# Sample attention: scores for four pages at once as rows instead of page by page as columns, key norms turned instead of scores, sequences written out on every engine

## The reference, cut to what matters

```python
k_nope = jnp.einsum('blc,chn->blhn', c, w_uk)
k = rms_norm(jnp.concatenate([k_nope, k_pe], axis=-1), g)
s = jnp.einsum('bqhd,blhd->bhql', q, k) * SM_SCALE
p = jax.nn.softmax(jnp.where(mask, s, -jnp.inf), axis=-1)
o_lat = jnp.einsum('bhql,blc->bqhc', p, c_all)
```

## Time and profile before

| | us |
|---|---|
| median of 3 runs | 3951.54 (3949.32 to 3975.61) |
| the profiled execution | 3975.4 |
| its span, first to last instruction | 3973.6 |
| PE busy, share of the span | 3224.3 (81%) |
| DVE busy | 2961.7 (75%) |
| ACT busy | 1041.3 (26%) |
| POOL busy | 1579.9 (40%) |
| mean granted PE clock, 1.0 is full speed | 0.872 |

### The profile page before, as it was taken

The page is one execution under the profiler, slowest core; times in us unless marked ns, Lnnn a source line. Parts: engine busy times, 40 slices in busy tenths (PEclk is TensorE's granted clock), DMA queues, the critical chain, the costliest instruction groups (busy, mean ns, idle before and its releaser), DMA issues. The chain is left out here.

```text
span 3973.6 us, 57296 instructions
## 1 busy us (share of the span) xinstructions
PE 3224.3 (81%) x19892; PEld 2722.2 (69%) x19892; DVE 2961.7 (75%) x5977; ACT 1041.3 (26%) x1915; POOL 1579.9 (40%) x1320
## 2 busy tenths in 40 slices
PE   6653787886999996665663768999999999999997
PEld 3443444654555554335662658999999999999997
DVE  3247686586665663775998996888888888888887
ACT  2221122222222221111212553222222222223221
POOL 0035354365333331663656772333333333333332
PEclk9577897576988997777886898999999999999998
DMA  2221775477876765882000338888888888888886
GB/s 105 102 92 39 273 266 198 136 256 247 262 248 219 230 197 172 306 321 81 27 17 23 158 152 296 307 300 300 294 297 296 296 291 294 304 300 293 292 301 237
DMA packets 303823, 876.76 MB, mean 221 GB/s; under 512 B 34009, under 2 KB 125450, under 8 KB 292554
## 3 DMA queue, kind: packets, MB, share of 16 engines
q0 software_dynamic: 147456, 536.94, 39.5%
q1 hardware_dynamic: 154170, 334.15, 23.4%
q10 hardware_dynamic: 2016, 3.67, 0.3%
HBM read 819.17 MB, written 55.74 MB: 220 GB/s over the span
## 5 line engine op out<-in xcount | busy, mean ns | idle before, releaser
L110 POOL DMA_INDIRECT x_got<-v,x_expert x512 | 548.9, 1072 | 969.1 <-DVE x_y L131 868.9
L110 POOL DMA_INDIRECT x_got<-u_rows,x_expert x512 | 566.6, 1107 | 854.6 <-DVE x_got L124 734.2
L131 DVE SCALAR_TENSOR_TENSOR x_y<-x_got,x_hidden,x_y 128x1024 f32<-128x1024 f32 x512 | 666.4, 1302 | 39.8 <-DMA x_got<-v,x_expert 29.9
L124 DVE SCALAR_TENSOR_TENSOR x_got<-x_got,x_y 128x1024 f32<-128x1024 f32 x512 | 621.1, 1226 | 37.8 <-DMA x_got<-u_rows,x_expert 36.1
L1682 PE MATMUL e_a<-h2h,e_uh 128*128 128x272 f32 x2048 | 591.0, 289 | 21.4 <-DVE e_ul L1760 20.8
L1684 PE MATMUL e_a<-h2h,e_ul 128*128 128x272 f32 x2048 | 594.3, 290 | 0.0
L1699 PE MATMUL e_y<-e_wh,e_vh 128*128 128x272 f32 x2048 | 588.3, 287 | 3.6 <-DVE e_wl L1783 3.6
L1683 PE MATMUL e_a<-h2l,e_uh 128*128 128x272 f32 x2048 | 589.6, 288 | 0.0
L1700 PE MATMUL e_y<-e_wl,e_vh 128*128 128x272 f32 x2048 | 588.2, 287 | 0.0
L1701 PE MATMUL e_y<-e_wh,e_vl 128*128 128x272 f32 x2048 | 587.3, 287 | 0.0
L1682 PEld LDWEIGHTS e_a<-h2h,e_uh 128*128 128x128 f32 x2048 | 386.6, 189 | 22.2 <-issue 21.1
(11 more groups left out here) (382 smaller groups left out, 5693.3 us busy)
## 6 DMA issues: line engine op xcount, KB each, us to landing
e_u<-uT SPq DMA_DIRECT2D x128, 512.0 KB
e_v<-v SPq DMA_DIRECT2D x64, 1024.0 KB
gates_d<-g_stage SPq DMA_DIRECT2D x8, 4352.0 KB
e_gate<-gates_d SPq DMA_DIRECT2D x32, 1088.0 KB
d_page<-page SPq DMA_DIRECT2D x128, 144.0 KB
d_latent<-page_rows SPq DMA_DIRECT2D x128, 128.0 KB
t0r_w<-w_pq SPq DMA_DIRECT2D x16, 512.0 KB
x_got<-u_rows,x_expert POOLq DMA_INDIRECT x512
```

What stands on the lines that cost most here:

```text
L110: pool.indirect_dma_start(out=self.got[n % RING_G][:], out_offset=None, in_=self.tables[phase], in_offset=bass.IndirectOffsetOnAxis(ap=sel ...
L124: dve.scalar_tensor_tensor(out=row[:], in0=row[:], scalar=1.0, in1=self.y[g][:], op0=ALU.mult, op1=ALU.mult, accum_out=self.hidden[:, g, k ...
L131: dve.scalar_tensor_tensor(out=self.y[g][:], in0=row[:], scalar=self.hidden[:, g, k:k + 1], in1=self.y[g][:], op0=ALU.mult, op1=ALU.add).t ...
```

## The change

- **Scores by rows.** After each fourth page PE makes the scores of four pages at once (`group`): the queries are the weights (128 by 32, and 32 by 32 for the rotary part), and four pages of keys are 512 columns. The result is 32 rows by 512 in one of two banks `sc`, which ACT copies to the score row (`raw`). The per-page matmuls into `st` and DVE's copies of them are gone.
- **Norms turned.** The reciprocal norms are spread to 32 columns for each page (`kinv`), and PE turns these instead of the scores, by matmuls with the identity. DVE multiplies the score row by them, bank by bank (`scaled`), before pages 2 and 3 of the next sequence.
- **New keys.** They are read in place; `k_new` and its copy are gone. The score row exists twice.
- **Loops.** All engines have the 8 sequences written out, with constant addresses.
- **Loads.** SP loads the next keys after the rotary squares and the fourth `raw` copy.

```diff
-        qr = sb("d_qr", [ROPE, H, NS])
-        qa = sb("d_qa", [P, CT, H, NS])
+        qr = sb("d_qr", [ROPE, DEC_B * SQ])
+        qa = sb("d_qa", [P, CT, DEC_B * SQ])
...
-        s_all2 = [sb(f"d_s{e}", [P, PAGES + 1, SQ]) for e in range(2)]
-        rows = sb("d_rows", [P, PAST + DEC_S])
-        s_row = rows[0:SQ, :]
+        kinv = sb("d_kinv", [P, PAGES, SQ])
+        s_new = [sb(f"d_snew{e}", [DEC_S, SQ]) for e in range(2)]
+        rows = [sb(f"d_rows{e}", [P, PAST + DEC_S]) for e in range(2)]
+        s_row = [r[0:SQ, :] for r in rows]
...
-        st = [bank("d_st0"), bank("d_st1")]
+        sc = [bank("d_sc0"), bank("d_sc1")]
...
+        def sequences(pages, tail):
+
+
+
+            before = {}
+            for b in range(DEC_B):
+                pages(b, b % 2, b // 2 + 1, before)
+                before = tail(b, b % 2, b // 2 + 1)
+            for step in before.values():
                 step()
...
-            with sp.Fori(0, DEC_B // 2 - 1) as m:
-                for e in range(2):
-                    n = 2 * m + e + 1
-                    sp.wait_ge(s["d_s1"], n)
-                    load_keys(n + 1, e)
-                    sp.wait_ge(s["d_lat"], n)
-                    load_latents(n + 1, e)
+            for n in range(1, DEC_B - 1):
+                e = (n - 1) % 2
+                sp.wait_ge(s["d_krsq"], n)
+                sp.wait_ge(s["d_raw"], GROUPS * n)
+                load_keys(n + 1, e)
+                sp.wait_ge(s["d_lat"], n)
+                load_latents(n + 1, e)
...
+                def group(c):
+
+                    after(pe, s["d_raw"], GROUPS * b + c - 1)
+                    o = sc[c % 2][0:SQ, :].rearrange("q (p l) -> q p l", l=P)
+                    four = slice(4 * c, 4 * c + 4)
+                    for k in range(CT):
+                        pe.matmul(o, qa[:, k, some], page[e][:, four, k * P:(k + 1) * P], start=k == 0, stop=False)
+                    pe.matmul(o, qr[:, some], krT[e][:, four, :], start=False, stop=True).then_inc(s["d_sc"], 1)
...
-                    after(pe, s["d_sev"], b * PAGES + p - 1)
                     for k in range(CT):
-                        pe.matmul(kn[p % 2][:, :], page[e][:, p, k * P:(k + 1) * P], w_uk[:, k, :],
-                                  start=k == 0, stop=k == CT - 1)
-                    for k in range(CT):
-                        pe.matmul(st[p % 2][:, 0:SQ].rearrange("p (h t) -> p h t", t=DEC_S),
-                                  page[e][:, p, k * P:(k + 1) * P], qa[:, k, :, cols], start=k == 0, stop=False)
-                    mm = pe.matmul(st[p % 2][:, 0:SQ].rearrange("p (h t) -> p h t", t=DEC_S),
-                                   krT[e][:, p, :], qr[:, :, cols], start=False, stop=True)
+                        mm = pe.matmul(kn[p % 2][:, :], page[e][:, p, k * P:(k + 1) * P], w_uk[:, k, :],
+                                       start=k == 0, stop=k == CT - 1)
                     mm.then_inc(s["d_mm"], 1)
+                    if p % 4 == 3:
+                        group(p // 4)
...
-                        pe.wait_ge(s["d_knew"], b + 1)
                         after(pe, s["d_smask"], b)
                         for h in range(H):
-                            mm = pe.matmul(new[0:DEC_S, h * DEC_S:(h + 1) * DEC_S], k_new[:, h, :],
-                                           qk_s[0:HD, h, bass.ds(b * DEC_S, DEC_S)], start=True, stop=True)
+                            mm = pe.matmul(new[0:DEC_S, h * DEC_S:(h + 1) * DEC_S], qk_s[0:HD, H + h, cols],
+                                           qk_s[0:HD, h, cols], start=True, stop=True)
...
-                def turn_first():
-
-                    pe.wait_ge(s["d_s1"], t + 1)
+                def norms_first():
+
+                    pe.wait_ge(s["d_kinv"], t + 1)
+                    after(pe, s["d_olT"], t)
+                    after(pe, s["d_pt"], 2 * t)
+                    norms(0)
+                    norms(1)
+
+                def norms(c):
+                    for p in range(4 * c, 4 * c + 4):
+                        mm = pe.matmul(misc[c % 2][0:SQ, (p % 4) * P:(p % 4 + 1) * P], kinv[:, p, :], ident[:],
+                                       start=True, stop=True)
+                    mm.then_inc(s["d_tr"], 1)
+
+                def norms_rest():
+                    for c in (2, 3):
+                        pe.wait_ge(s["d_nb"], GROUPS * t + c - 1)
+                        norms(c)
                     pe.wait_ge(s["d_smask"], t + 1)
-                    pe.wait_ge(s["d_olT"], t)
-                    pe.wait_ge(s["d_pt"], 2 * t)
-                    turn(0)
...
-                        mm = pe.transpose(misc[c % 2][0:SQ, (p % 4) * P:(p % 4 + 1) * P], s_all[:, p, :], ident[:])
-                    mm.then_inc(s["d_tr"], 1)
-
-                def turn_rest():
-                    for c in (2, 3):
-                        pe.wait_ge(s["d_row"], 5 * t + c - 1)
-                        turn(c)
-                    pe.transpose(new[0:SQ, 2 * SQ:2 * SQ + DEC_S], s_all[0:DEC_S, PAGES, :],
-                                 ident[0:DEC_S, 0:DEC_S]).then_inc(s["d_tr"], 1)
+                    pe.transpose(new[0:SQ, 2 * SQ:2 * SQ + DEC_S], s_new[e][:],
+                                 ident[0:DEC_S, 0:DEC_S]).then_inc(s["d_ntr"], 1)
...
-                return {1: turn_first, 2: turn_rest, 6: probs, 7: latent, 9: latent_turn}
-            sequences(pe, lambda b: None, pages, tail)
...
+                    if p % 4 == 3:
+                        c = p // 4
+                        act.wait_ge(s["d_sc"], GROUPS * b + c + 1)
+                        after(act, s["d_ptr"], 2 * (b - 1))
+                        act.activation(s_row[e][:, 512 * c:512 * c + 512], sc[c % 2][0:SQ, :],
+                                       ACT.Copy).then_inc(s["d_raw"], 1)
...
-                    act.activation(s_row[:, 512 * c:512 * c + w],
-                                   misc[c % 2][0:SQ, 0:w] if c < 4 else new[0:SQ, 2 * SQ:2 * SQ + w],
-                                   ACT.Copy).then_inc(s["d_row"], 1)
...
+                def row_new():
+                    act.wait_ge(s["d_ntr"], t + 1)
+                    act.activation(s_row[e][:, PAST:PAST + DEC_S], new[0:SQ, 2 * SQ:2 * SQ + DEC_S],
+                                   ACT.Copy).then_inc(s["d_nrow"], 1)
...
-                return {2: rows_first, 3: rows_rest, 5: exp, 7: probs, 10: latent_turn}
-            sequences(act, lambda b: None, pages, tail)
+                return {3: row_new, 5: exp, 7: probs, 10: latent_turn}
...
-            dve.tensor_scalar(qr[:], qk_s[NOPE:HD, 0:H, 0:NS], g_k[NOPE:HD, :], None,
+            dve.tensor_scalar(qr[:].rearrange("p (b h t) -> p h b t", b=DEC_B, h=H),
+                              qk_s[NOPE:HD, 0:H, 0:NS].rearrange("p h (b t) -> p h b t", b=DEC_B), g_k[NOPE:HD, :], None,
                               ALU.mult).then_inc(s["d_qg"], 1)
 
-            def begin(b):
-                after(dve, s["d_new"], b)
-                dve.tensor_copy(k_new[:], qk_s[0:HD, H:2 * H, bass.ds(b * DEC_S, DEC_S)]).then_inc(s["d_knew"], 1)
-                after(dve, s["d_tr"], 5 * (b - 1))
...
-                    dve.wait_ge(s["d_mm"], b * PAGES + p + 1)
-                    dve.tensor_copy(s_all[:, p, :], st[p % 2][:, 0:SQ]).then_inc(s["d_sev"], 1)
                     gather.step(dve, steps[p])
...
-                dve.wait_ge(s["d_sev"], (b + 1) * PAGES)
-                sv = s_all[:, 0:PAGES, :].rearrange("p k (h t) -> p (k h) t", t=DEC_S)
-                dve.tensor_tensor(sv, sv, kss[:].rearrange("p k h -> p (k h)").unsqueeze(2)
-                                  .to_broadcast((P, PAGES * H, DEC_S)), ALU.mult).then_inc(s["d_s1"], 1)
+                after(dve, s["d_tr"], GROUPS * b)
+                dve.tensor_copy(kinv[:].rearrange("p k (h t) -> p (k h) t", t=DEC_S),
+                                kss[:].rearrange("p k h -> p (k h)").unsqueeze(2)
+                                .to_broadcast((P, PAGES * H, DEC_S))).then_inc(s["d_kinv"], 1)
 
             def tail(t, e, n):
+                def scaled(c):
+                    cols = slice(512 * c, 512 * c + 512)
+                    dve.wait_ge(s["d_raw"], GROUPS * t + c + 1)
+                    dve.wait_ge(s["d_tr"], GROUPS * t + c + 1)
+                    dve.tensor_tensor(s_row[e][:, cols], s_row[e][:, cols], misc[c % 2][0:SQ, :],
+                                      ALU.mult).then_inc(s["d_nb"], 1)
...
                 def maximum():
-                    dve.wait_ge(s["d_row"], 5 * t + 5)
-                    dve.tensor_reduce(mx[:], s_row, AX, ALU.max).then_inc(s["d_mx"], 1)
+                    dve.wait_ge(s["d_nb"], GROUPS * t + GROUPS)
+                    dve.wait_ge(s["d_nrow"], t + 1)
+                    dve.tensor_reduce(mx[:], s_row[e], AX, ALU.max).then_inc(s["d_mx"], 1)
...
-                return {4: maximum, 9: latent}
-            sequences(dve, begin, pages, tail, True)
```

(7 more changed lines are left out.)

74 lines of the change are left out of this document (27 added, 47 removed).

## The result

The changed kernel took **4031.46 us** (median of 4 runs, 4014.13 to 4050.38) against 3957.6 us for the kernel before (4 runs as well, one more than in the table above): ratio 1.0181, 95% interval 1.011 to 1.0253. The forecast was 3899.5, and the range, 3868 to 3934, does not hold the result. The profiled execution took 4047.02 us, with a span of 4045.2.

A forecast was written before the change was run, and what follows sets the result against it. PE was taken as the bound, busy 509.65 of sample attention's 565 us. Six shorter periods (-44.8), sequence 0 (-7.3) and sequence 7 (0) gave -52 us, so 3899.5 us, range 3868 to 3934.

The forecast's parts named there:

- rival D: PE, with more written-out code, waits for instructions; would eat half the gain: 3925 us, chance 0.03.
- Sample attention, -52: Whole forecast gain, all in sample attention: six periods 44.8 us, sequence 0 7.3 us, sequence 7 nothing.
- A group, 2.56: PE's scores of four pages: six records of 512 columns at 0.427 us, 2.56 us; four pages 9.40 instead of 10.44.
- rival C: Slower: groups read four pages in strides, a record costs 0.85 us; +30 us in all, 3982 us, chance 0.05.
- Norms turned, 3.4: PE's 16 norm turns per sequence as full f32 matmuls, 32 records of 0.107 us: 3.4 us, +1.7.
- New keys' scores, 0.54: PE's new keys' scores at each sequence, written out: 0.54 us instead of 1.08 with register addresses.
- Wait at the meeting: Between sequences, PE's 3.5 us wait for `k_new` goes, and with it the 1.6 us fall of the clock.
- Rival B: Wait at the meeting of sequences stays because DVE or the gather becomes late: 3935 us, chance 0.17.
- Waits within a period, 3.1: PE's waits in one sample attention period (scaled bank, `kinv`, probabilities, output turn): 3.1 us instead of 1.5.
- Clock at the probabilities, 3.8: Loss by PE's fallen clock around the probabilities, per period: 3.8 us taken, where 4.9 stood in five sequences.
- Rival A: The clock holds throughout once the long wait is gone: period 56.6 us, total 3876 us, chance 0.1.
- Period 60.4: One sample attention period: pieces 53.4, waits 3.1 and clock 3.8 us, giving 60.4 instead of 67.9.

The follow-up runs named there:

- the written-out runs: Kernel before with PE's and ACT's sample attention loops written out, 64 idle PE instructions ahead of the experts' loop: 3960.82 us, ratio 0.9989.
- shifts by 24 and by 200: Idle PE instructions ahead of the experts' loop: 24 in the kernel before, 4036.25 us; 200 in the changed kernel, 4006.79 us.
- +80 instructions: Kernel before with 80 idle PE instructions ahead of the experts' loop: 3979.43 us, ratio 1.0013.
- +48: Kernel before with 48 idle PE instructions ahead of the experts' loop: 4041.25 us, ratio 1.0183.
- the run with new keys in place: Kernel before, sample attention written out on PE and ACT, idle PE instructions before experts, new keys read without copy or its wait: 3935.39 us, ratio 0.9932.

## Why the prediction was wrong

**The step that failed** is the one under rival D: "PE, with more code, waits for instructions. Against: sequences 0 and 7 were written out and show no such gap", with a chance of 0.03 and 3925, and with it the sum's silence on all other stages. The argument looked for the cost in the code that was written out. There it is nothing, as the written-out runs show. The cost stands 850 us later: experts +118.3 us, 88.2 of them in 13 stops, one behind each jump back of a loop that nobody touched and whose place in PE's program the change moved by 4.3 blocks, from x.69 to x.99. Nothing in the trace of before shows how near that loop is to the edge, but what would have raised the question was there: q8 with 64 packets, a loop of 1598 instructions passed 14 times, and a change that adds 1102 instructions ahead of it. A body of 6.24 blocks touches 8 from 24% of all starts. So a tenth to a quarter was the honest chance for a loss that I could not have sized, and it would have ended on the other side, slower.

The Trainium skill (Runtime: NRT & Kernel Launch, section "Instruction fetch mechanics") says that TensorE's instruction memory holds 2048 instructions, refilled in blocks of 256, that is 8 blocks. The runs agree with that size if the block that is fetched ahead counts too: 7 touched and one ahead stay, 8 and one ahead make the 9 packets of a pass. The same section says that a jump to a place outside the current window of two blocks makes the engine wait. The runs do not agree there: the kernel before jumps back over 6 blocks in each pass, without a packet and without a stop.

The other steps, each with what the trace of the change has:

- **Sample attention, -52:** -45.8. The mechanism was right, the size near: six periods -42.5 (forecast -44.8), the stretch up to sequence 1 -5.1 (-7.3), from the last meeting to the next stage +1.9 (0).
- **A group, 2.56:** 2.81, and four pages 9.87 instead of 9.40. The records do pass at the keys' pace (six in 2.81; rival C needed 0.70 a record), but each change of kind costs a step, as 0.11 did before. Pages in a row took 1.77 each, not 1.71, and pages that stand alone between other matmuls 1.91. In a period: +3.
- **Norms turned, 3.4:** 3.7. **New keys' scores, 0.54:** as said.
- **Wait at the meeting, gone, with its slow clock:** right, in 6 of 7 meetings no wait and once 0.56. Rival B falls for the change, though with the scores still by pages a part of it was true (1.26).
- **Waits within a period, 3.1:** 0.93. The 0.8 for the scaled bank and the 0.2 to 0.3 for `kinv` did not come, the 1.5 before the probabilities were 0.67, the 0.5 before the output's turn 0.26. -2.2.
- **Clock at the probabilities, 3.8:** 3.3, by page 7 at 3.71 for 1.91, the group behind it 3.43 for 2.81, and the turning 4.56 for 3.7; the latents ran at full clock. Rival A falls.
- **Period 60.4:** 60.9 in four, 61.6 and 59.4 in the other two, 60.8 on the mean. That it is so near is in part luck: the steps between kinds of matmul (+3) and the waits (-2.2) nearly cancel.
- **Range:** the prediction's bounds of the clock give 3887 and 3907 by its own sum; its 3912 does not follow from them. Nothing hangs on that.

Without the loop's place, the changed kernel came to a ratio of 0.9898 and 0.9913; 52 us of 3951.54 would be 0.9868, which lies inside the first interval and just outside the second.

## What to carry to other kernels

A change that adds or removes instructions on an engine moves every later loop of that engine's program, and a long loop body (here 1598 instructions on PE) can fall out of the instruction memory with nothing of its work changed: before believing that a change is slower, compare untouched stages, and look for idle time put down to "issue" at the head of each pass and for packets on the engine's instruction queue in steady state. A loop of this size is better written out, or kept so short that even the worst start leaves it within 7 blocks (not tried here); a few idle instructions ahead of it are the cheap test. And a faster part ahead of partners with fixed queues turns into waits: of 2 us saved in turning, 1.6 came back as waits, and moving the waiter a page on laid bare one wait that its work had covered.

## What was not expected of the hardware

- A jump back that waits for one instruction block stands still for 2.2 to 4.2 us (3.2 on the mean, shifts by 24 and by 200), one that waits for two for 5.6 to 8.1 (6.8 on the mean), with the DMA engines 0.79 busy in the stretch shown, and the clock is low for some records behind it. Of the 118.3 us, 88.2 are idle, and the other 30, 2.3 a pass, go with records of 0.59 and 0.43 instead of 0.28.
- The edge is sharp: the kernel before at +0 and +80 instructions takes 1549.4 us for its experts, at +24 1611.5, at +48 1623.0.
- Neighbouring periods with the same instructions and the same waits can differ by 4.8 us in 60.6 with only the granted clock differing; in the last four periods of the run with new keys in place they alternate (60.61, 65.45, 60.60, 65.51).

Open are where the 0.15 block (some 40 instructions) between the counted and the true place comes from, and whether a body of another length has its edge where the sum says: only the place was varied, never the length. Best of all versions, within what their intervals tell, are the changed kernel with experts written out and the two with transposed turns, one at a good place and one with experts written out: 0.9856 to 0.9862 of the time before.
